# Output projection, norm and routing of a decoder layer, written out for 16 tiles, with routing for pairs of tiles

## Reference

```python
mixed = jnp.concatenate([_rmsnorm(attn, g_attn), _rmsnorm(lru, g_lru)], axis=-1)
h = _layernorm(ALPHA * x + mixed @ w_out, ln1_g, ln1_b)      # (z - mean) * rsqrt(var + eps) * g + b
scores = jax.nn.sigmoid(h @ w_router)                        # 2048 x 64 experts
sel = scores + e_bias
group_score = lax.top_k(sel.reshape(n, 8, 8), 2)[0].sum(-1)  # best two of each group of 8
gidx = lax.top_k(group_score, 4)[1]                          # 4 of 8 groups allowed
_, idx = lax.top_k(jnp.where(emask, sel, -jnp.inf), 8)       # 8 experts of the allowed groups
wts = scores[idx] / scores[idx].sum() * 2.5
```

## Time and profile before

| | |
|---|---|
| median of 3 executions | 2754.09 us (2744.99 to 2757.0) |
| profiled execution, its own time | 2761.0 us |
| its span in the trace | 2758.8 us |
| busy share of the span: TensorE, VectorE, ScalarE, GpSimd | 93%, 56%, 43%, 26% |
| `output_and_route` in the trace | from about 640 to 921 us |
| mean granted TensorE clock | 0.96 of full speed |

### The profile page before, as it was taken

One profiled execution on the slowest core, in us unless ns is written; L12 is line 12 of the kernel. 1 busy time (PEld: TensorE's weight loads), 2 busy tenths in 40 slices (PEclk: granted clock), 3 DMA queues, 4 the chain that ended last, 5 costly groups with the idle time before them and its releaser, 6 DMA issues. The chain is left out here.

```text
span 2758.8 us, 50465 instructions
## 1 busy us (share of the span) xinstructions
PE 2568.1 (93%) x11861; PEld 1979.8 (72%) x11863; DVE 1548.6 (56%) x2691; ACT 1181.7 (43%) x1791; POOL 725.6 (26%) x824
## 2 busy tenths in 40 slices
PE   8999999997899499899999999999999999999990
PEld 4655656465777387688888888888888888888880
DVE  2444435254888687565566555565655555665525
ACT  2424344254333211454455454454545444554425
POOL 0000000001121200243334433344333333443335
PEclk9999898998999699999999999999999999999995
DMA  5010101005343654788789888798888878988657
GB/s 183 4 58 0 61 0 34 26 8 211 124 151 112 203 170 144 234 250 242 218 247 282 259 227 235 207 288 259 249 255 255 241 205 239 275 253 236 166 114 266
DMA packets 257636, 495.90 MB, mean 180 GB/s; under 512 B 28480, under 2 KB 170816, under 8 KB 257600
## 3 DMA queue, kind: packets, MB, share of 16 engines
q1 hardware_dynamic: 206640, 313.22, 33.4%
q0 software_dynamic: 47808, 179.59, 26.1%
q10 hardware_dynamic: 3152, 2.66, 0.3%
HBM read 365.89 MB, written 129.53 MB: 180 GB/s over the span
## 5 line engine op out<-in xcount | busy, mean ns | idle before, releaser
L1808 POOL DMA_INDIRECT acc<-y,si x164 | 295.3, 1801 | 776.4 <-DMA acc<-y,si 337.9
L1897 DVE TENSOR_TENSOR gu_lo<-raw_gu,gu_hi (+1 forms) x128 | 292.7, 2287 | 175.0 <-ACT gu_hi L1828 158.4
L2005 PE MATMUL psG<-gu_hi,xT_lo 128*128 x1320 | 348.4, 406 | 1.9 <-DVE xT_lo L1894 1.3
L1994 PE MATMUL psG<-gu_hi,xT_hi 128*128 x1328 | 338.3, 397 | 3.1 <-ACT xT_hi L1824 3.1
L1994 PE MATMUL psG<-gu_lo,xT_hi 128*128 x1328 | 336.0, 395 | 0.0
L1994 PEld LDWEIGHTS psG<-gu_hi,xT_hi 128*128 128x128 f32 x1328 | 250.5, 189 | 64.1 <-issue 3.8
L1994 PEld LDWEIGHTS psG<-gu_lo,xT_hi 128*128 128x128 f32 x1328 | 249.7, 188 | 60.2
L2005 PEld LDWEIGHTS psG<-gu_hi,xT_lo 128*128 128x128 f32 x1320 | 236.6, 189 | 47.0 <-issue 2.9
L1828 ACT ACTIVATE gu_hi<-raw_gu (+1 forms) x128 | 238.2, 1909 | 45.3 <-issue 45.3
L623 PE MATMUL psP<-xT,win 128*128 128x512 f32 x512 | 235.9, 618 | 3.5 <-DMA win<-in_w_in_dram 3.5
L1897 DVE TENSOR_TENSOR d_lo<-raw_d,d_hi (+1 forms) x64 | 146.7, 2293 | 151.5 <-ACT d_hi L1828 151.5
(11 more groups left out here) (290 smaller groups left out, 3889.5 us busy)
## 6 DMA issues: line engine op xcount, KB each, us to landing
raw_gu<-in_w_gate_dram SPq DMA_DIRECT2D x64, 1024.0 KB
raw_gu<-in_w_up_dram SPq DMA_DIRECT2D x64, 1024.0 KB
raw_d<-in_w_down_dram SPq DMA_DIRECT2D x64, 1024.0 KB
xs<-in_x_dram SPq DMA_DIRECT2D x20, 512.0 KB, 4.3
htab<-row SPq DMA_DIRECT2D x16, 544.0 KB, 2.7
mT<-mixed SPq DMA_DIRECT2D x16, 512.0 KB, 5.4
xt<-in_x_dram SPq DMA_DIRECT2D x16, 512.0 KB, 5.9
hT_d<-hT SPq DMA_DIRECT2D x16, 512.0 KB, 3.8
```

Source lines behind the costliest of these rows:

```text
L1808: nc.gpsimd.indirect_dma_start(out=acc, out_offset=bass.IndirectOffsetOnAxis(ap=si[k][:, 0:1], axis=0), in_=y[k][:], in_offset=None, compu ...
L1897: nc.vector.tensor_tensor(dst, src, hi, ALU.subtract).then_inc(dlo_s if n == 2 else gulo_s, 1)
L1994: nc.tensor.matmul(psG[slot][:], xT_hi[slot][:, c, :], right[:, bass.ds(w, 1), c, :].rearrange("p a n -> p (a n)"), start=(n == 0 and c == ...
L2005: m = nc.tensor.matmul(psG[slot][:], xT_lo[slot][:, c, :], gu_hi[:, bass.ds(w, 1), c, :].rearrange("p a n -> p (a n)"), start=False, stop= ...
```

## The change

What it does, part by part:

- **Written out.** The hardware loops are gone; all 16 tiles are straight code. The order on VectorE for tile n is: add the recurrent half of tile n - 1, statistics, centre, one half of a pair's routing, norm of n - 1, low part of n + 1, add the attention half of n, another half of a pair's routing.
- **Low parts** `mT_lo` are made by VectorE instead of GpSimd.
- **Norm.** `nmr`, ScalarE's `zn` and the two tensor_tensor operations give way to two fused ones on VectorE: (z - mean) * gain, which doesn't wait for rstd, and that times rstd + bias.
- **Routing for pairs** of tiles (seven pairs, then tiles 14 and 15 each alone, behind the last norm). Every operation works on two tiles' 128 scores; the best two of a group are found as the greatest of all sums of two members (a 128x512 add and a 128x512 reduce), not by eight max operations; one operation makes the mask from the rank, and one applies it.
- **First tile** of the projection: TensorE starts with the high parts of w_out as they come, instead of waiting for four low parts.
- **Stores.** The state goes out when the norm is done (4096 bytes of a row), the weights on their own for a pair (256 bytes of a row), `hT` when it is made; SyncE's loads no longer stand behind the weights of a tile.
- ScalarE scales `xt` in place (no `xa` buffer) and reads psT and psR as before.

```diff
         @block.sync
+            load_mixed(2)
+            for n in range(TILES + 1):
+                if n:
+                    store_h(n - 1)
+                if n + 3 < TILES:
+                    load_mixed(n + 3)
+                if n + 2 < TILES:
+                    load_x(n + 2)
+                if n:
+                    store_hT(n - 1)
+                if n % 2 == 0 and n >= 4:
+                    store_weights(n // 2 - 2)
...
         @block.gpsimd
-                nc.gpsimd.tensor_tensor(mT_lo[s.slot][:], mT[s.slot][:], mT_hi[s.slot][:], ALU.subtract).then_inc(mlo_s, 1)
-            two_deep(pool, TILES, low, rsqrt)
+            for n in range(TILES):
+                pool.wait_ge(stat_s, 3 * n + 3)
...
+                nc.gpsimd.tensor_tensor(rstd[:], ve[:], nhalf[:], ALU.pow).then_inc(rstd_s, 1)
...
         @block.scalar
-            two_deep(act, TILES, (head, nothing, normalise), (turned, scores))
+            scale_x(0)
+            for n in range(TILES + 1):
+                if n + 1 < TILES:
+                    high(n + 1)
+                    scale_x(n + 1)
+                if n:
+                    turned(n - 1)
+                    scores(n - 1)
...
         @block.vector
+            def centre(n):
+                dve.wait_ge(stat_s, 3 * n + 3)
+                nc.vector.scalar_tensor_tensor(out=z[:], in0=z[:], scalar=mv[:, 0:1], in1=gain[:],
+                                               op0=ALU.subtract, op1=ALU.mult).then_inc(zg_s, 1)
+            def norm(n):
+                dve.wait_ge(zg_s, n + 1)
+                dve.wait_ge(rstd_s, n + 1)
...
+                nc.vector.scalar_tensor_tensor(out=h[n % 2][:], in0=z[:], scalar=rstd[:], in1=bias[:],
+                                               op0=ALU.mult, op1=ALU.add).then_inc(h_s, 1)
+            def group_scores(r):
...
+                link(nc.vector.tensor_tensor(sel[:, 0:G, :, :], bcast(s, 2, 2), bcast(b, 2, 2), ALU.add))
...
+                link(nc.vector.tensor_tensor(pairs[:, 0:G, :, :], bcast(first, 2, EG_SIZE // 2), partner, ALU.add))
+                link(nc.vector.tensor_reduce(gs[:, 0:w, :].rearrange("p t g -> p (t g)"),
+                                             pairs[:, 0:G, :, :].rearrange("p g s e -> p g (s e)"), AX.X, ALU.max))
...
-            two_deep(dve, TILES, (head, factors, gain_bias), (group_best, group_order, choose))
+            low(1)
+            add_attention(0)
+            for n in range(1, TILES + 1):
+                r = (n - 3) // 2
+                add_lru(n - 1)
+                statistics(n - 1)
+                centre(n - 1)
+                if n >= 3:
+                    (group_scores if n % 2 else allowed)(r)
+                norm(n - 1)
+                if n + 1 < TILES:
+                    low(n + 1)
+                if n < TILES:
+                    add_attention(n)
+                if n >= 3:
+                    (group_order if n % 2 else weights)(r)
+            for r in range(len(routes) - 2, len(routes)):
+                group_scores(r)
+                group_order(r)
+                allowed(r)
+                weights(r)
...
         @block.tensor
-            two_deep(pe, TILES, (head, last_half), (turn, route))
+            first_tile()
+            for n in range(1, TILES):
+                attention(n)
+                lru(n, 0)
+                turn(n - 1)
+                lru(n, 1)
+                route(n - 1)
+            turn(TILES - 1)
+            route(TILES - 1)
```

More of the change, by code:

```diff
@@ L947, in _ @@
[L947 to L956, removed]
@@ L1018, in _ @@
                 if c == 0:
[L1019 to L1023, removed]
-                s.wait_slot(act, xt_in, per=16)
-                s.wait(act, z1_s, behind=1)
-                nc.scalar.activation(xa[:], xt[s.slot][:], ACT.Copy, scale=ALPHA).then_inc(xa_s, 1)
-            def normalise(s):
-                s.wait(act, nmr_s)
-                nc.scalar.activation(zn[:], z[:], ACT.Identity, scale=rstd[:], bias=nmr[:]).then_inc(zn_s, 1)
@@ L1033, in turned @@
-            def turned(s):
-                s.wait(act, hTps_s)
-                act.wait_ge(hT_out[s.slot], 16 * s.turn)
-                nc.scalar.activation(hT[s.slot][:], psT[:], ACT.Copy).then_inc(hT_s, 1)
-            def scores(s):
-                s.wait(act, logit_s)
-                s.wait(act, w_s, behind=1)
-                nc.scalar.activation(sc[:], psR[:, 0:EXPERTS], ACT.Sigmoid).then_inc(sc_s, 1)
-            two_deep(act, TILES, (head, nothing, normalise), (turned, scores))
+                    high(0)
@@ L1077, in factors @@
-            def factors(s):
-                s.wait(dve, pool_s, per=2)
-                s.wait(dve, stat_s, per=3)
-                nc.vector.scalar_tensor_tensor(out=nmr[:], in0=mv[:, 0:1], scalar=-1.0, in1=rstd[:],
-                                               op0=ALU.mult, op1=ALU.mult).then_inc(nmr_s, 1)
-            def gain_bias(s):
-                s.wait(dve, zn_s)
-                dve.wait_ge(row_out[s.slot], 16 * s.turn)
-                nc.vector.tensor_tensor(row[s.slot][:, 0:D], zn[:], gain[:], ALU.mult).then_inc(zg_s, 1)
-                s.wait(dve, zg_s)
-                nc.vector.tensor_tensor(row[s.slot][:, 0:D], row[s.slot][:, 0:D], bias[:], ALU.add).then_inc(h_s, 1)
@@ L1091, in chain @@
-            def chain(s, done):
-                def link(ins):
-                    nonlocal done
-                    done += 1
-                    ins.then_inc(topk_s, 1)
-                    dve.wait_ge(topk_s, s.n * TOPK_STEPS + done)
-                    return done
-                return link
-            def group_best(s):
-                link = chain(s, 0)
-                s.wait(dve, sc_s)
-                link(nc.vector.tensor_tensor(sel[:], sc[:], ebias[:], ALU.add))
-                carry_wait(dve, passed)
-                for e in range(EGROUPS):
-                    last = nc.vector.max(g8[:, e, :], sel[:, e * EG_SIZE:(e + 1) * EG_SIZE])
-                link(last)
@@ L1172, in half @@
-            def half(s, acc, k0, h):
-                for n, (left, right) in enumerate(((mT_hi, wo_hi), (mT_hi, wo_lo), (mT_lo, wo_hi))):
-                    if n == 2 and k0 == 0 and h == 0:
-                        s.wait(pe, mlo_s)
-                    for k in range(4):
-                        m = nc.tensor.matmul(acc[:, h, :], left[s.slot][:, k0 + k, :], right[:, k0 + k, h * 512:(h + 1) * 512],
-                                             start=(n == 0 and k == 0), stop=(n == 2 and k == 3))
-                return m
@@ L1181, in last_half, with half @@
-            def last_half(s):
-                half(s, psL, 4, 1).then_inc(proj_s, 1)
-            def turn(s):
+            passes = ((mT_hi, wo_hi), (mT_hi, wo_lo), (mT_lo, wo_hi))
+            def half(n, acc, k0, hf):
+                for part, (left, right) in enumerate(passes):
+                    for k in range(k0, k0 + HALF):
+                        m = nc.tensor.matmul(acc[:, hf, :], left[n % 2][:, k, :], right[:, k, hf * 512:(hf + 1) * 512],
+                                             start=(part == 0 and k == k0), stop=(part == 2 and k == k0 + HALF - 1))
+                return m
```

339 lines of the change are left out of this document (203 added, 136 removed).

## The result

Six runs of the changed kernel have a median of 2732.3 us (2722.9 to 2734.1), six of the kernel before beside them 2751.8: a ratio of 0.9902 with an interval of 0.9881 to 0.9923, so 27 us or 1.0% faster (21 to 33 by the interval). The two medians themselves are only 19.5 us apart (0.9929, just outside that interval); how the recorded ratio weighs the runs isn't on record. The repeat further down gives 0.9905 by the same reckoning and 28.5 us between its medians, so I take the gain as 20 to 28 us. Forecast were 0.9905 and 2728 us, with 2716 to 2742 as the range. The profiled execution took 2726.3 us, its span is 2724.5.

The account below looks back on a forecast made before the run. VectorE was taken to bound the block at 15.45 us a tile, TensorE next at 13.71. Last second add -24.9, tail -0.3, next block -1 made -26.2 us: ratio 0.9905, 2728 us, range 2716 to 2742.

Parts of the forecast that it names:

- The bound: In the block before the change, VectorE sets the pace of 15.45 us a tile; TensorE is next at 13.71.
- The stall: VectorE's bias add takes 3.29 us instead of 1.22 in every tile, held 2.07 us by GpSimd's low part.
- VectorE's sum of 12.05: VectorE's work per tile after the change: 8.45 us plus 3.6 for routing; bounds 11.5 to 13.8.
- The order: In steady tiles VectorE's norm is done 2.0 us before TensorE wants it, so TensorE runs through.
- The rule against it: GpSimd's `ve` and `rstd` meet VectorE's centre: h some 1.2 us later, VectorE's sum 13.25, tile still 13.71 us.
- First tile, +2.9 us: The projection's first tile costs 0.5 to 2.9 us more; the upper value takes TensorE's slow start as now.
- Tail, -0.3: From the last second add to the last weights: 20.6 us instead of 20.9.
- Next block, -1: At the next block's start, the first `hT` load has no two stores in front: 0 to -2 us, taken as -1.
- The sum: Last second add -24.9, tail -0.3, next block -1: in all -26.2 us, profiled execution 2761.0 to 2734.8.
- VectorE as the bound (2): In steady tiles VectorE still sets the pace, 14.55 to 15.0 us a tile, 2744 to 2750 us; chance 0.09.
- Straight code (3): Fetching TensorE's straight code leaves gaps: 17.9 or 20.0 us a tile, about 2791 or 2822 us; chance 0.03.
- That the change frees more (4): TensorE at full pace from the first tile, shorter next-block start: -31 us, 2723; chance 0.86 together with TensorE becoming the bound.

Follow-up runs that it names:

- The repeat: The changed kernel once more, unchanged, timed again beside the kernel before: 2732.7 us, ratio 0.9905.
- a_cutpe: The changed kernel without the pass mT_hi by wo_lo for tiles 1 to 15 (output differs slightly): 2690.6 us, ratio 0.9746 to the kernel before.
- b_unrolled: The kernel before with the block's hardware loops written out, nothing else changed: 2748.0 us, ratio 0.9943.
- b_lowdve2: The kernel before, loops kept, with the low parts moved to VectorE ahead of the first add: 2743.6 us, ratio 0.9932.
- b_unr_lowdve: The kernel before with loops written out and low parts on VectorE ahead of the first add: 2731.8 us, ratio 0.9889.
- a_single: The changed kernel with routing tile by tile in place of pairs: 2733.1 us, ratio 0.9904 to the kernel before.
- a_lowpool: The changed kernel with the low parts back on GpSimd: 2733.0 us, ratio 0.9887 to the kernel before.

## Why the prediction was right

**The bound.** VectorE set the pace, TensorE was next with 13.71 us a tile. Right: 13.68 in the steady tiles, at a clock of 1.00, and a_cutpe shows that TensorE is what holds it there.

**The stall.** GpSimd's low part costs VectorE 2.07 us a tile. Right in kind and size (b_unrolled keeps it, b_lowdve2 lacks it), but the row was misread: the bias add isn't held in every tile. In the kernel before, the bias add (3.29 us) and `gm`, an operation over 8 columns, are held by turns. `gm`, in two tiles in a row:

```profile
800.18 2.11 DVE L1128 TENSOR_SCALAR gm<-grank 128x8 f32<-128x8 f32 x1
...
818.00 0.17 DVE L1128 TENSOR_SCALAR gm<-grank 128x8 f32<-128x8 f32 x1
```

That costs 2.07 us in one tile and 1.94 in the next. As a reason of the gain it is one of two: written-out loops bring 0.93 us a tile, the low parts' move 1.14, and I had priced the loops' share only as gaps in passing.

**VectorE's sum of 12.05.** Too high, and outside its bounds of 11.5 to 13.8: 11.1 measured. Centre and norm take 1.285 us (forecast 1.28), but the next operation starts 1.20 us after their start where I had 1.32, and the same holds for the low part (1.13, I had 1.26) and the first add (1.19, I had 1.43). A pair's routing takes 6.87 us (forecast 7.2), and the gaps of 0.15 that I took from the earlier trace rows are gone in straight code: centre starts 0.25 us after the aggregate's start, I had 0.36. So VectorE waits 2.3 to 2.9 us a tile where I had 1 to 2, and is busy 39.8 in the window where I had about 44. None of this reaches the time, because TensorE's sum is the higher one.

**The order.** The norm was to end 2.0 us ahead of the transposes. It ends at 781.67, they start at 784.18: 2.5.

**The rule against it.** `ve` lost its turn to centre: 1.31 instead of 0.22 us. `rstd` (0.60) then is ready at 779.33, the norm starts at 780.39 and doesn't wait. Only in the first two tiles, without routing between centre and norm, does it wait, 0.85 us. The Trainium skill, SBUF — State Buffer, "Who interferes with whom", says of such a pair of instructions that the one that starts first keeps the other out for its whole length; here VectorE was first, so the price fell on GpSimd, and the trace agrees with the 1.31. For `rstd` no such price shows: it runs across `sel` and `pairs`, two VectorE operations with two inputs in SBUF, takes 0.60 us (0.57 before), and they take 0.42 and 0.69, the durations of the forecast. So the 1.2 us that the forecast added to VectorE's sum for this case (13.25) didn't come.

**First tile, +2.9 us.** This term was mis-sized: it is +0.5. I had taken the slow start of the earlier trace rows over. The changed kernel's windows there:

```profile
650.00:660.00 10.00, 7.30 (x16) 4.04 (x16) 6.94 (x6) 5.51 (x7) 0.00 (x0) 0.51 1.00 387
660.00:670.00 10.00, 10.00 (x46) 8.19 (x45) 5.63 (x7) 2.12 (x2) 0.29 (x1) 1.00 1.02 360
```

TensorE had work for 7.3 of the 10 us ahead of 660, at half clock. Its matmuls from the last `wo_hi` blocks on:

```profile
656.58 2.17 PE L1220 MATMUL psL<-wo_hi,mT_hi 128*128 128x512 f32 x4 [1.89 <-ACT wo_hi L1040]
658.55 2.61 PE L1220 MATMUL psA<-wo_lo,mT_hi 128*128 128x512 f32 x8
661.00 1.99 PE L1220 MATMUL psL<-wo_lo,mT_hi 128*128 128x512 f32 x8
```

The last cast of `wo_hi` ends at 657.47 and the tile's last matmul at 666.7, 9.2 us later, where I had 10.2: full pace came in the middle of the eight from 658.55 on, not behind twelve slow ones. That is 1.0 of the 2.4 us. The other 1.4 are the blocks themselves: the last pair of casts starts 11.7 us after the first cast, in the kernel before 13.1 (658.27 - 645.17). The first second add comes 23.0 us after the first `wo_hi` cast in place of 22.5.

**Tail, -0.3.** 19.3 us (870.19 to 889.48) against 20.9: -1.6. Counted from the last second add, the norm is done at 7.1 us (forecast 8.0), the last pair's weights at 9.0 (10.2) and tile 14's at 14.0 (15.4). The scores of tile 15 were earlier than I had them too, or they would have taken that back: VectorE waits 0.28 us for them and starts at 884.44, 14.3 us after the last second add.

**Next block, -1.** The load of `hT` takes 4.7 us from issue to its use, before 7.1, and the first gate/up comes 23.0 us after the block's end instead of 25.9: -2.9. Of that 2.3 are the load, the right cause at more than twice the price; the load takes 6.9 and 6.6 us in b_unrolled and b_unr_lowdve, which keep the old stores, and 4.7 to 5.1 in the changed kernel's repeat and a_single, which have the new ones. Another 0.6 is that it is issued sooner after the last weights (0.7 us instead of 1.3).

**The sum.** From the first cast of w_out on: pace 203.4 instead of 231.7 us, -28.3 (forecast -27.8); first tile +0.5 (+2.9); tail -1.6 (-0.3); next block -2.9 (-1); rest -0.6. That is -32.9 against -26.2 forecast, and with 1.4 us that the block started earlier it is the 34.3 us between the two spans. The timed runs show 27 by the recorded ratio (21 to 33), 19.5 between the plain medians and 28.5 in the repeat. So the forecast, made from a trace, missed the traces by 7 us and hit the timed runs. Part of that is luck: the profiled pair, 34.7 us apart, lies above what the interval allows, and the forecast's errors at the first tile, the tail and the next block are all on one side, which the timed runs don't show; from the first second add on, the repeat's trace saves 30.9 us. Where the rest between traces and timed runs is lost is open.

**The rivals.** VectorE as the bound (2): refuted. VectorE idles, the 0.15 us more on each link are absent in b_unrolled and a_cutpe, and the exclusion cost GpSimd's `ve` the time and not VectorE. Straight code (3): refuted, TensorE has no gap in 50 us with all 16 tiles written out. That the change frees more (4): in the traces it came true (-32.9 us, it had said -31), by a cheaper first tile and a shorter start of the next block; the timed runs don't settle it.

## What to carry over

- Work out, stage by stage, which engine sets the pace and the sum of the engine that comes next. What takes time off the first one pays only down to the second's sum: here two parts of the change filled all of it, and pairs and the fused norm made VectorE idle more. Which part "did it" has no answer of its own: the low parts' move was worth 1.1 us a tile before the loops were written out, and nothing that a_lowpool could show beside all the rest.
- Ask of each moved operation who waits for it and what stands ahead of it in its new engine's order. Behind the norm the low part cost 6 us a tile, ahead of the first add it gained 1.1.
- A large GpSimd operation in SBUF can hold what VectorE runs beside it; look for that by VectorE's small operations that take over 2 us, also in the block behind. Not every one is held: in a_lowpool the `MAX8` and `MATCH_REPLACE8` at 770.89 to 771.77 take what they take in the changed kernel (0.35 us for two `MAX8`, 0.21 for a replace) beside the low part that runs from 770.82 on.

## What was not expected of the hardware

- Hardware loops cost 0.93 us of a 15.45 us tile of some thirty VectorE operations: 0.15 to 0.2 us at each of several waits of VectorE on its own last operation, 0.6 at the turn (every second tile), and these are gone in straight code. That it is the waits on register values which cost this is likely, not shown.
- Exclusion between VectorE and GpSimd goes both ways. `ve` went from 0.22 to 1.31 us under centre, and in b_unrolled the low part takes 3.44 where it took 2.54. There the low part and the bias add start together: the bias add takes its own 1.22 us, the low part ends late, and the next operation to be held is `gm`, 2.11 instead of 0.17. GpSimd, then VectorE, in b_unrolled:

```profile
778.93 3.44 POOL L990 TENSOR_TENSOR mT_lo<-mT,mT_hi 128x1024 fp32r<-128x1024 f32 x1 [2.93 <-ACT mT_hi L1013]
```

```profile
778.90 1.22 DVE L1089 TENSOR_TENSOR row<-row,bias 128x1024 f32<-128x1024 f32 x1
...
780.29 2.11 DVE L1128 TENSOR_SCALAR gm<-grank 128x8 f32<-128x8 f32 x1
```

- After 7.3 us of work in 10 at a granted clock of 0.51, so at or near the level of 1.2 GHz, TensorE ran the next 10 us at 1.00, 2.4 GHz.
